# A two-block network on one core: the recurrent stage reordered around its gates, and identity products in TensorE's waits

## The reference

```python
gate_br, xb = jnp.split(x @ w_in, 2, axis=-1)          # w_in 1024 x 2048
xc = conv(xb, 4 taps)
r = sigmoid(xr @ w_rgate + b_rgate)                    # 2 directions x 4 blocks of 256 x 256
i = sigmoid(xr @ w_igate + b_igate)
a = exp(-8 * r * softplus(-lam)); mult = sqrt(-expm1(2 * log a)); u = mult * i * xc
h = scan_forward(a[0], u[0]) + scan_backward(a[1], u[1])
out = (h * gelu(gate_br)) @ w_out                      # then x = layer_norm(alpha * x + out)
```

## Time and profile before

| | us |
|---|---|
| median of 3 runs | 1637.2 (1635.61 to 1640.09) |
| the profiled execution's own time | 1640.99 |
| its span | 1639.7 |
| TensorE busy | 1171.5 (71%) |
| VectorE, ScalarE, GpSimd busy | 471.4, 300.0, 65.8 |

### The profile page before, as it was taken

How to read it: one execution, slowest core, us unless ns; L and a number is a source line. 1 busy time by engine, 2 the same in 40 slices (tenths; PEclk the granted TensorE clock), 3 DMA queues, 4 the chain that set the end, 5 groups by cost and what they waited for, 6 DMA issues and landing times.

```text
span 1639.7 us, 18312 instructions
## 1 busy us (share of the span) xinstructions
PE 1171.5 (71%) x7977; PEld 630.2 (38%) x7977; DVE 471.4 (29%) x984; ACT 300.0 (18%) x598; POOL 65.8 (4%) x88
## 2 busy tenths in 40 slices
PE   7998855678476565795875566656555499987887
PEld 6655411144121111783541111111111188543883
DVE  4444301101111002747430100000100467554524
ACT  4430100000310000463110000000000154340520
POOL 2000100000000000021000000000000100001000
PEclk9899878799798778797997877876878799998899
DMA  9605999999999999363799999999999722106310
GB/s 358 270 1 187 417 427 427 422 416 420 424 426 426 423 426 403 115 231 125 263 423 427 425 424 428 423 427 425 423 427 424 286 84 103 52 13 245 131 52 26
DMA packets 89664, 503.29 MB, mean 307 GB/s; under 512 B 6914, under 2 KB 15568, under 8 KB 56816
## 3 DMA queue, kind: packets, MB, share of 16 engines
q1 hardware_dynamic: 84224, 492.78, 73.7%
q10 hardware_dynamic: 3680, 8.04, 1.5%
q0 software_dynamic: 1680, 1.30, 0.2%
HBM read 501.00 MB, written 1.10 MB: 306 GB/s over the span
## 4 chain that ended last, share of the span: by engine, by line
DMA 49%; PE 37%; DVE 7%; ACT 4%; issue 1%; POOL 1%; ACTq 0%; SPq 0%; DVEq 0%
DMA weight_ring<-in_moe_w_gate_up 29%; DMA weight_ring<-in_moe_w_down 17%; PE bank L411 7%; PE bank L1251 4%; PE bank L328 3%; PE bank L329 3%; PE bank L330 3%; PE bank L1278 2%; DMA weight_spare<-in_ada_w 2%; DVE weight_ring_rounded L368 1%; PE bank L2200 1%; PE bank L647 1%; PE bank L631 1%; PE bank L825 1%; PE bank L661 1%
## 5 line engine op out<-in xcount | busy, mean ns | idle before, releaser
L1251 PE MATMUL bank<-weight_ring,expert_tokens 128*32 128x512 f32 x2048 | 324.7, 769 | 205.3 <-DMA weight_ring<-in_moe_w_gate_up 199.4
L1251 PEld LDWEIGHTS bank<-weight_ring,expert_tokens 128*32 128x32 f32 x2048 | 66.8, 126 | 435.4 <-DMA weight_ring<-in_moe_w_gate_up 251.8
L1278 PE MATMUL bank<-weight_ring,actT 128*32 128x256 f32 x2048 | 167.6, 486 | 77.6 <-DMA weight_ring<-in_moe_w_down 68.7
L1369 DVE TENSOR_TENSOR act<-silu,bank 128x256 f32<-128x256 f32 x32 | 13.4, 420 | 440.1 <-ACT silu L1417 440.1
L1278 PEld LDWEIGHTS bank<-weight_ring,actT 128*32 128x32 f32 x2048 | 77.1, 134 | 156.0 <-DMA weight_ring<-in_moe_w_down 66.2
L1374 DVE COPY expert_outs<-bank 32x256 f32<-32x256 f32 x64 | 26.7, 418 | 267.8 <-PE bank L1278 266.8
L1417 ACT ACTIVATE silu<-bank 128x256 f32<-128x256 f32 x32 | 12.3, 384 | 487.1 <-PE bank L1251 487.1
L368 DVE TENSOR_TENSOR weight_ring_rounded<-weight_ring,weight_ring_rounded 128x1024 fp32r<-128x1024 f32 (+1 forms) x68 | 79.1, 1224 | 33.2 <-ACT weight_ring_rounded L352 32.9
L1426 ACT COPY expert_outs<-bank 32x256 f32<-32x256 f32 x64 | 23.3, 365 | 235.0 <-PE bank L1278 234.2
L352 ACT CAST weight_ring_rounded<-weight_ring 128x1024 fp32r<-128x1024 f32 (+1 forms) x64 | 61.9, 1046 | 8.0 <-DMA weight_ring<-in_attn_w_qkv 7.5
L447 POOL TENSOR_TENSOR norm_rstd<-norm_var,minus_half 128x1 f32<-128x1 f32 x12 | 18.3, 1527 | 961.0 <-DVE norm_var L435 961.0
(11 more groups left out here) (442 smaller groups left out, 1809.2 us busy)
## 6 DMA issues: line engine op xcount, KB each, us to landing
weight_ring<-in_moe_w_gate_up SPq DMA_DIRECT2D x128, 2048.0 KB, 30.8
weight_ring<-in_moe_w_down SPq DMA_DIRECT2D x64, 2048.0 KB, 31.1
weight_ring<-in_ada_w SPq DMA_DIRECT2D x8, 2048.0 KB, 14.2
weight_ring<-in_even_w_in SPq DMA_DIRECT2D x5, 2048.0 KB, 15.2
weight_ring<-in_odd_w_in SPq DMA_DIRECT2D x5, 2048.0 KB, 8.1
weight_spare<-in_ada_w SPq DMA_DIRECT2D x4, 2048.0 KB, 19.8
weight_ring<-in_lru_w_in SPq DMA_DIRECT2D x4, 2048.0 KB, 25.7
weight_ring<-in_attn_w_qkv SPq DMA_DIRECT2D x2, 2048.0 KB, 15.3
```

The costliest lines, as they stand in the source:

```text
L1251: last = pe.matmul(up[CAP * j:CAP * (j + 1), :], B.xs[:, t, e * CAP:(e + 1) * CAP], w[:, t % 2, :, j, :], start=(t == 0), stop=(t == T - 1))
L1278: last = pe.matmul(K[3][CAP * q:CAP * (q + 1), 0:QC], B.actT[i][:, s, j * CAP:(j + 1) * CAP], w[:, jj, s, q, :], start=(j == 0 and s == 0) ...
```

## The change

- `units()`: in the recurrent stage the seven slots now take lru2, lru2_hi, lru3, lru3_hi, rgate, igate, lru0; lru0_hi follows in lru2's slot, then decay_room (lru2_hi's), lru1 (lru3's), lru1_hi (lru3_hi's), lru_out0 (rgate's), lru_out1 (igate's). The turn of slots for the second mixture changes with it: its first units wait for lru0_hi, decay_room and lru1, its first ada units for lru1_hi and lru0.
- TensorE forms the gates of both directions right behind lru2 and lru3, in pairs of blocks (rgate 0, 1, igate 0, 1, rgate 2, 3, igate 2, 3), and projects lru0 and lru1 behind them.
- ScalarE rounds lru2 before it rounds x, rounds lru0 and lru1 before the sigmoids, and makes all four gelus at the end, behind root(1).
- VectorE does one pair of x and one chunk of lru2 by turns, splits lru0 and lru1 behind the convolution, and in direction 1 adds and multiplies each tile right behind its scan.
- The decay rates are computed inside the first mixture, at experts 3 and 4.
- The out product of the first half of the tokens takes both 512-column blocks of a feature tile before the next tile, in all four stages that use it.
- `idle_products_tensor` issues products of the identity with itself into a bank whose content is not used: 36 at the end of each mixture, 12 behind the turning of x in the recurrent stage, 12 before and 16 behind the transposes of the even stage, 36 before and 16 behind those of the odd stage.

```diff
@@ units()
+            first = [state["slots"][(state["at"] + i) % SLOTS] for i in range(SLOTS)]
+            for name, i in (("lru2", 0), ("lru2_hi", 1), ("lru3", 2), ("lru3_hi", 3), ("rgate", 4), ("igate", 5), ("lru0", 6),
+                            ("lru0_hi", 0), ("decay_room", 1), ("lru1", 2), ("lru1_hi", 3), ("lru_out0", 4), ("lru_out1", 5)):
+                put(name, first[i])
+            state["slots"], state["at"] = [first[i] for i in (0, 1, 2, 3, 6, 4, 5)], 0
@@ Program
+    def idle_products_tensor(self, bank, n):
+        for _ in range(n):
+            self.pe.matmul(bank[:, 0:P], self.B.ident, self.B.ident, start=True, stop=True)
@@ out_product_tensor
+            for j, c in [(j, c) for j in range(T) for c in range(2)] if half == 0 else [(j, c) for c in range(2) for j in range(T)]:
+                if half == 0 and c == 0:
+                    pe.wait_ge(*sig.after(*y_event(j)))
+                last = pe.matmul(banks[2 * half + c], y[:, j, rows], w[c][:, j], start=(j == 0), stop=(j == T - 1))
@@ experts_tensor, at its end
+        self.idle_products_tensor(K[5], 36)
@@ experts_vector, experts_scalar
+            if layer == 0 and e == 4:
+                self.rates_vector()
...
+            if layer == 0 and e == 3:
+                self.rates_scalar()
@@ recurrent_tensor
+    GATE_ORDER = [(unit, n) for pair in ((0, 1), (2, 3)) for unit in ("rgate", "igate") for n in pair]
...
         self.turn_x_tensor("recurrent", K)
+        self.idle_products_tensor(K[5], 12)
...
-        inputs("lru2", 0, 0)
-        inputs("lru3", 4, 2)
-        inputs("lru0", 0, 4)
-        gates(0, 6)
-        gates(1, 14)
-        inputs("lru1", 4, 22)
+        inputs("lru2", 0)
+        inputs("lru3", 2)
+        gates(0, 4)
+        gates(1, 12)
+        inputs("lru0", 20)
+        inputs("lru1", 22)
@@ recurrent_vector
+        for pair in range(T // 2):
...
+            v.tensor_tensor(flat(B.lru_lo), K[pair], flat(B.lru_hi), ALU.subtract).then_inc(
+                *sig.tell("x_split", ("features", "recurrent", pair)))
+            v.wait_ge(*sig.after("rounded", "lru2", pair))
+            v.tensor_tensor(lo[:, c], raw[:, c], hi[:, c], ALU.subtract).then_inc(*sig.tell("weights_split", ("weights", "lru2", pair)))
...
-        self.split_weights_vector("lru2")
         self.split_weights_vector("lru3")
-        self.split_weights_vector("lru0")
...
@@ recurrent_vector, scans(z), in the loop over f
+                if z == 1:
+                    v.wait_ge(*sig.after("scanned", 1, f))
+                    v.tensor_tensor(B.R[0][:, f, :], B.R[0][:, f, :], B.R[1][:, f, :], ALU.add).then_inc(*sig.tell("lru_outputs"))
+                    v.wait_ge(*sig.now("lru_outputs"))
+                    v.wait_ge(*sig.after("gelu", f // 2))
+                    v.tensor_tensor(B.R[0][:, f, :], B.R[0][:, f, :], B.gelu[:, f, :], ALU.mult).then_inc(
+                        *sig.tell("lru_outputs", ("y", "recurrent", f)))
...
+        self.split_weights_vector("lru0")
+        self.split_weights_vector("lru1")
         decays(0)
-        self.split_weights_vector("lru1", rounded_here=True)
         scans(0)
         decays(1)
         scans(1)
@@ recurrent_scalar
+        self.split_weights_scalar("lru2")
+        self.split_x_scalar("recurrent", K, B.lru_hi)
+        self.split_weights_scalar("lru3")
         self.norm_rows_scalar("recurrent")
...
+        inputs("lru2", 0, 0)
+        self.split_weights_scalar("lru0")
+        inputs("lru3", 4, 2)
+        self.split_weights_scalar("lru1")
+        gates(0, 4)
         decays(0)
-        gates(1, 14)
+        gates(1, 12)
         root(0)
-        inputs("lru1", 4, 22)
         decays(1)
         root(1)
+        inputs("lru0", 0, 20)
+        inputs("lru1", 4, 22)
@@ even_tensor
+        self.idle_products_tensor(K[5], 12)
         self.modulated_tensor("even", K)
+        self.idle_products_tensor(K[5], 16)
```

More of the change, by code:

```diff
@@ L273, in units @@
         if layer == 0:
-            for name in ("lru2", "lru3", "lru0"):
-                put(name)
-                put(f"{name}_hi")
-            put("rgate")
-            put("igate")
-            put("decay_room")
-            put("lru1")
-            put("lru1_hi")
-            put("lru_out0")
-            put("lru_out1")
+            first = [state["slots"][(state["at"] + i) % SLOTS] for i in range(SLOTS)]
[3 more added lines that the diff above has]
+            state["slots"], state["at"] = [first[i] for i in (0, 1, 2, 3, 6, 4, 5)], 0
     state["slots"], state["at"] = [0, 1, 2], 0
@@ L400, in out_product_tensor @@
         sig, pe = self.sig, self.pe
+        w = [self.plain(name).rearrange("p (t c) -> p t c", t=T) for name in names]
         for half in range(H):
+            rows = slice(half * P, (half + 1) * P)
             for c in range(2):
[L403 to L404 removed]
                 if free[2 * half + c] is not None:
@@ L1482, in recurrent_tensor @@
-        gates(0, 6)
-        gates(1, 14)
-        inputs("lru1", 4, 22)
+                lru_free(job)
+                pe.wait_ge(*sig.after("arrived", unit))
+                for ff in range(2):
+                    for c in range(2):
+                        pe.wait_ge(*sig.after("conv", 2 * n + c))
+                        at = c * LBW + ff * P
+                        last = pe.matmul(self.lru_bank(job)[:, ff * S:(ff + 1) * S], w[:, z * LB + n, at:at + P], B.xc[:, 2 * n + c],
+                                         start=(c == 0), stop=(c == 1))
@@ L1561, in recurrent_vector @@
         scans(1)
-        for f in range(T):
-            v.wait_ge(*sig.after("scanned", 1, f))
-            v.tensor_tensor(B.R[0][:, f, :], B.R[0][:, f, :], B.R[1][:, f, :], ALU.add).then_inc(*sig.tell("lru_outputs"))
-            v.wait_ge(*sig.now("lru_outputs"))
-            v.wait_ge(*sig.after("gelu", f // 2))
-            v.tensor_tensor(B.R[0][:, f, :], B.R[0][:, f, :], B.gelu[:, f, :], ALU.mult).then_inc(
-                *sig.tell("lru_outputs", ("y", "recurrent", f)))
         self.residual_vector("recurrent", K)
```

107 lines of the change are left out of this document (48 added, 59 removed).

## The result

The changed kernel takes 1622.93 us in the median of four runs (1618.47 to 1625.44), the kernel before 1638.64 (four runs beside it): ratio 0.990 [0.9883, 0.9918]. The same kernel timed again, and once more with a change that turned out to be worth nothing, gave 0.9882 [0.9859, 0.9904] and 0.9898 [0.9882, 0.9914]. The mean of the three, 0.9893, is 17.5 us less. The forecast was 22.2 less, 1615 against the median; the time lies in its range of 1606 to 1627, but above the 1610 to 1620 that the forecast's own chance stood for, beside the numbers of rivals A and B (1622, 1623 to 1625). The mean ratio on the forecast's base of 1637.2 gives 1619.7, just inside. The profiled execution took 1618.47 us (span 1617.2), 22.5 less than the profiled one of before; that this meets the forecast is partly luck, as shown further down.

A forecast was written before the change was run, and what follows sets the result against it. The prediction took the second mixture to be bound by its weight stream's start and the last two stages by the engines; -18.0 - 2.3 - 1.9 = -22.2 gave 1618.8 profiled, 1615 against the median, range 1606 to 1627.

The forecast's parts named there:

- rival A: Clock not held across transposes and sparse first products; first projections run low, 3 us late in recurrent stage: 1622, chance 0.12.
- Rival B: Recurrent stage's long chain slower: lru1 lands 4 us later, scans and decays(1) take 4 more: 1623 to 1625; 0.12 shared.
- The bound: Second mixture is bound by its weight stream; only the start of the steady stream, set by the recurrent stage, counts there.
- both dates: Start of second mixture's stream: last scan at 755.3 releases five units, landed by 783.3; ada slots come free from 778.6.
- The recurrent stage: From x to the second mixture's stream: the steady stream comes 18.0 us earlier.
- The cast of lru1: ScalarE ahead of the sigmoids: lru1 lands 8.3 us after issue, as igate was, at 697.0; four casts end at 700.9.
- The period of a tile: VectorE in direction 1: scan of 0.6, addition and multiplication of about 0.4 each, one y each 1.45 us.
- Even and odd: Last two stages: shorter transposes, 1.6 us each, and first projections, 0.7 and 0.3: -2.3 and -1.9.
- Identity products: TensorE's waits: 0.26 us each (0.24 to 0.46), fitting the waits with at most 0.2 us delay and keeping the clock full.
- The rule on transposes: Rule against the change: transposes don't count as clock activity, so the clock could fall in or just behind them.

The follow-up runs named there:

- early_ada: slots_mid with the second mixture's first ada unit loaded into the first freed slot and multiplied ahead of the out product: 1608.37 us, 0.9818.
- after_again: The changed kernel timed again with no edit, against the kernel before: 1619.38 us, 0.9882.
- no_idle: The changed kernel with all six calls for identity products taken out: 1622.05 us, 0.9898 of the kernel before.
- out_order: The changed kernel with the out product's first half of tokens in the old order, block by block over all tiles: 1622.41 us, 0.9898.
- double: The changed kernel with 72 identity products instead of 36 at the end of each mixture: 1630.26 us, 0.9957.
- mid_split: The changed kernel with ScalarE rounding lru1 behind direction 0's sigmoids instead of ahead of all sigmoids: 1617.52 us, 0.986.
- slots: The changed kernel with another turn of slots for the second mixture, decay_room's slot going to the second ada unit: 1619.76 us, 0.9879.
- y_loop: The changed kernel with direction 1's additions and multiplications by gelu back behind its eight scans: 1620.19 us, 0.9879.
- slots_mid: The changed kernel with the edits of slots and mid_split together: 1613.1 us, 0.9836 of the kernel before.
- slots_mid_noidle: slots_mid without identity products in any stage: 1617.33 us, 0.9868 of the kernel before.
- idle_only: The kernel before with only the six calls for identity products added at the same places: 1638.2 us, 1.000.

## Why the prediction was right, point by point

**The bound** was right: T to back follows the start of the steady stream. The ten changed kernels of the table ahead of early_ada fit a rule of two dates. Where the bytes are late (after, after_again, no_idle, out_order, double, mid_split), T to back is the first ada issue plus 512.5, 510.9, 510.8, 510.9, 512.7 and 513.2 us. Where the ada slots are late (slots, y_loop, slots_mid, slots_mid_noidle), it is the fourth ada issue plus 489.4, 488.6, 487.9 and 490.2; the three kernels in the old order fit that too (486.8, 488.0, 489.6). The two distances are read off these same kernels, but which date binds can be seen without them: in the second group the transfers stand still behind the queued units (0.02 at 773 to 783 in slots, 0.09 at 778 to 784 in y_loop, 0.08 at 764 to 774 in slots_mid, 0.01 at 771 to 778 in slots_mid_noidle), in the first they don't. The later of the two decides, within some 2 us. In after itself the two dates lie within about 1 us of each other by this rule, so that an edit on either alone can give little. The prediction had both dates, and that the bytes bind after the change.

**The recurrent stage.** Forecast -18.0, measured from T to back: 612.4, 610.5 and 612.1 in three profiles of after and its like, 628.1 and 627.5 in two of before, so -16.2. The steps, each against T:
- First product 4.4 behind T, forecast 3.8. Pairs every 1.73 us, forecast 1.8. lru3 finished and lru1 issued 29.9 behind T, forecast 30.0.
- The cast of lru1 starts 10.6 behind the unit's issue, forecast 8.3 from igate. This is the first mis-sized term, 2.2 us against T (40.5 against 38.3), and all of ScalarE's gate work is queued behind it. The trace of before had a nearer row, lru1 itself, which landed 8.9 after its issue. Rival B named this place; it came at about half its size, and the other half of B (4 more in the scans and decays(1)) didn't come.
- From there the sum held: the table loads stand 7.3, 7.8 and 7.3 apart; root(1) came 82.9 behind T (81.0 forecast), the first out product 89.4 (87.3).
- The period of a tile was 1.52 us, not 1.45, as a scan takes 0.68, not 0.60: in the row of eight in 4.76 us the next one starts 0.58 to 0.60 behind the last, before that has ended, and between other operations it doesn't. Last scan over 99.0 behind T against 96.6.
- The out product took 30.77, forecast 30.70.
- The five units landed without a gap, and the fourth ada issue was hidden behind them, as forecast. 

**Even and odd.** Forecast -2.3 and -1.9. Even, from the transposes to the copy of cq behind the first projection: 17.55, 16.34, 16.39 and 16.26 us in the four profiles without identity products, 14.50 to 15.64 in the ten with them, mean 15.0 against 16.6: -1.6. Odd, from transposes to out product: 88.8 in all four without them, 86.4 to 90.2 in the ten with them, mean 87.5: -1.3. By the traces both terms are some 0.6 too large. For even it is less still if the whole way from transposes to out product is taken, 169.3 against 170.3 on average, since the later part of that stage varies by itself (see the last section). The timed comparisons agree only loosely: idle_only gives 0 [-2.6, +2.8], no_idle against after 1 to 3 (0.8 against the mean ratio, 2.6 against after_again, timed beside it), slots_mid against its twin 5. That the products bring 2 to 3 us in the whole time is likely and not shown.

**Identity products.** 0.228 us each, just below the forecast's 0.24 to 0.46, and all in their waits; `double` shows what they cost beyond. What the forecast had wrong is that they hold the clock to the end of the first projection. In the recurrent stage they did so in five of the nine executions in the new order that have them, and there lru1 went out 29.8 to 29.9 behind T. In the other four (slots, y_loop, out_order, early_ada) the clock fell for some 3 us right behind the sparse first products, and lru1 went out at 31.4 to 31.6; without any products, at 32.3 and 32.5. In slots:

```profile
669.00:673.00 4.00, 3.85 (x19) 3.86 (x20) 4.00 (x7) 0.00 (x0) 0.00 (x0) 0.57 0.02 7
```

At the cast little of this is left, as the transfer takes between 8.7 and 11.1 us from execution to execution: 39.6 to 40.5 where the clock held, 41.1 to 42.7 where it fell, 41.0 and 41.3 without products. In even the clock fell behind the transposes in nine of the ten executions with the products, in odd in eight. So rival A was in part right: its event came, often, at about half its price in the recurrent stage (1.6 of 3 us), and it takes off part of the gain in even and odd, not all of it.

**The rule on transposes.** In no_idle the clock was 0.50 for the 4 us before the transposes, with TensorE idle, and 1.00 right behind them, with nothing but the sixteen instructions of the turn in between. In other executions the same sixteen instructions behind an idle TensorE left it at 0.50, here in the even stage of before:

```profile
1303.00:1308.00 5.00, 3.38 (x16) 3.28 (x16) 2.80 (x8) 0.46 (x1) 1.44 (x2) 0.50 0.53 200
1308.00:1312.00 4.00, 0.30 (x2) 0.00 (x0) 2.94 (x7) 4.00 (x9) 0.00 (x0) 0.50 0.00 0
```

Of the twelve such starts in the four kernels without identity products the clock rose in five and stayed low in seven. The Trainium skill, TensorE: Matmul & The Clock Gate, section Part 4: PE-mode transpose, says that transposes don't count as activity for the clock. The five starts don't agree with that for these fp32 turns, which the kernel writes as `pe.transpose` and the trace shows as one product with the identity for each block. Whether the falls that rival A needs are due to the transposes or to the sparse products behind them, these runs don't tell apart.

**The sum.** -16.2 - 1.6 - 1.3 = -19.1 by the traces, -17.5 by the timings (each ratio is uncertain by 0.2%, 3 us); forecast -22.2. The terms that were too large are the stage (lru1's wait 2.2, less what is given back behind it, the tile's period 0.5) and even and odd (0.7 and 0.6). That the two profiled executions differ by 22.5 is luck: the one of before ran 2.4 us above its median, the one of after 4.5 below.

## What to carry to other kernels

When a stream of weights must restart behind a stage, write down every date that can hold it (bytes still to land, slots still to be freed) and move the later one; here an edit on the earlier one alone measured as 1 us of the mixture's end, another as 4, and the two together as 9. Then take bytes out of the restart: one unit of 2.1 MB used in a wait ahead of it gave 5 us here. And before two traces are compared, find the first date on the chain that moves by itself, here the arrival of one unit, and count from it: in one experiment 2.2 of 3.0 us that looked like the edit's were that date's. Filler products are free only up to the wait that they fill, so their price per product should be read from the trace and counted against what is left of that wait.

## What the runs showed that was not expected

- The last unit of lru_w_in came at 287 GB/s in its main stretch, and its cast started 10.6 us behind its issue:

```profile
690.00:694.00 4.00, 4.00 (x20) 3.52 (x19) 4.00 (x6) 0.00 (x0) 0.00 (x0) 1.00 0.98 287
```

 The transfers' busy share is 0.98 there: they are busy and move less. From issue to cast the same unit took between 8.7 and 11.1 us in the eleven executions in the new order, and it landed in 8.9 in before. What sets this isn't shown.
- The even stage has a coin of its own: from the copy of cq to the out product it took 153.2 to 153.3 us in seven of the fourteen profiles and 154.6 to 155.0 in the other seven, whatever the kernel. In the stretch in which they part, the granted clock was 0.79 in after and 1.00 in no_idle; such a second fall of the clock stands there in six of the seven longer executions (in the seventh, double, the first fall is longer) and in none of the shorter ones:

```profile
1436.00:1444.00 8.00, 6.26 (x21) 3.36 (x21) 4.30 (x13) 2.51 (x6) 0.00 (x0) 0.79 0.00 0
```

```profile
1434.30:1442.30 8.00, 6.26 (x25) 2.99 (x24) 5.26 (x15) 2.51 (x6) 0.00 (x0) 1.00 0.00 1
```

- Identity products right behind the transposes don't always hold the clock: in the even stage of after it was 0.61 at 1288 to 1292, with TensorE busy all of the 4 us:

```profile
1288.00:1292.00 4.00, 4.00 (x25) 4.00 (x24) 2.46 (x6) 2.66 (x6) 0.00 (x0) 0.61 0.26 93
```
